# Hybrid encoder layer: first weight units, keys and six rounds of the expert choice moved into the stages before them

## The reference, cut to what matters

```python
proj = _rmsnorm(x, norm_mix) @ w_in            # GLA q, k, v, gate, decay codes; attention q, k, v; z_a, z_b
o_a = _gla_branch(...)                         # 4 heads, forward and backward scans in chunks
o_b = _gqa_branch(...)                         # 8 query heads, 2 key/value heads, softmax
merged = sigmoid(z_a) * (o_a @ w_o_gla) + sigmoid(z_b) * (o_b @ w_o_att)
x = x + merged @ w_out
h = _rmsnorm(x, norm_ffn)
aff = softmax(h @ w_router)                    # 16 experts, per group of tokens
gate_vals, idx = top_k(aff.T, cap)             # cap = 128 of the sample, 32 of the prompt
hid = silu(h[idx] @ w_e_gate) * (h[idx] @ w_e_up)
x = x.at[idx].add((hid @ w_e_down) * gate_vals)
```

## Time and profile before

| | |
|---|---|
| time, median of 3 runs (lowest to highest) | 3313.82 us (3312.66 to 3315.59) |
| the profiled execution: own time; its span | 3316.98 us; 3315.1 us |
| PE busy (matmuls) | 3036.5 us, 92% |
| DVE busy; ACT busy; POOL busy | 1709.4; 1522.0; 566.2 us |
| mean granted TensorE clock | 0.962 |
| DMA | 600.82 MB, mean 181 GB/s |

### The profile page before, as it was taken

How to read it: one execution, slowest core, us unless ns; L and a number is a source line. 1 busy time by engine, 2 the same in 40 slices (tenths; PEclk the granted TensorE clock), 3 DMA queues, 4 the chain that set the end, 5 groups by cost and what they waited for, 6 DMA issues and landing times. The chain is left out here.

```text
span 3315.1 us, 51547 instructions
## 1 busy us (share of the span) xinstructions
PE 3036.5 (92%) x19370; PEld 2396.8 (72%) x19370; DVE 1709.4 (52%) x1712; ACT 1522.0 (46%) x1635; POOL 566.2 (17%) x726
## 2 busy tenths in 40 slices
PE   7999998988888699979692999999999999999998
PEld 6888885766666589968572777777777777777776
DVE  3101001454432289942225767676676676666765
ACT  4211112445532166631342566665665565656654
POOL 0048881112220000000100011111100011111100
PEclk9999998999999799989895999999999999999999
DMA  4324322233215200024533788887777888878774
GB/s 153 122 98 142 119 89 96 84 100 103 90 61 179 92 20 19 13 91 144 173 127 129 267 296 288 285 298 272 280 279 287 298 287 285 302 272 297 277 280 155
DMA packets 196331, 600.82 MB, mean 181 GB/s; under 512 B 15184, under 2 KB 45536, under 8 KB 196256
## 3 DMA queue, kind: packets, MB, share of 16 engines
q1 hardware_dynamic: 165616, 506.46, 42.7%
q0 software_dynamic: 21920, 76.03, 7.7%
q10 hardware_dynamic: 8720, 17.30, 1.5%
HBM read 522.33 MB, written 77.33 MB: 181 GB/s over the span
## 5 line engine op out<-in xcount | busy, mean ns | idle before, releaser
L1871 DVE TENSOR_TENSOR ex_w_lo<-ex_w_raw,ex_w_hi 128x2048 fp32r<-128x2048 f32 x384 | 879.9, 2292 | 451.1 <-ACT ex_w_hi L1826 451.1
L1826 ACT ACTIVATE ex_w_hi<-ex_w_raw 128x2048 fp32r<-128x2048 f32 x381 | 729.9, 1916 | 469.6 <-PE ex_ps_s L1958 469.5
L1958 PE MATMUL ex_ps_s<-ex_w_hi,ex_xS 128*128 128x512 f32 x2048 | 578.2, 395 | 0.0
L1958 PEld LDWEIGHTS ex_ps_s<-ex_w_hi,ex_xS 128*128 128x128 f32 x2048 | 375.9, 188 | 99.4 <-issue 26.3
L1958 PE MATMUL ex_ps_s<-ex_w_lo,ex_xS 128*128 128x512 f32 x1024 | 316.4, 390 | 0.0
L1958 PE MATMUL ex_ps_s<-ex_w_hi,ex_hidS 128*128 128x512 f32 x1024 | 307.9, 403 | 0.0
L1812 POOL DMA_INDIRECT y<-ex_ye_s,ex_rows_y x16 | 43.5, 2717 | 1147.3 <-DVE ex_ye_s L1914 1147.3
L1969 PE MATMUL ex_ps_p<-ex_w_raw,ex_xP 128*32 128x256 f32 x4096 | 236.0, 383 | 0.0
L108 PE MATMUL pj_ps_tok<-pj_w_hi,act_hl 128*128 128x512 f32 x560 | 219.2, 391 | 8.6 <-DVE pj_w_lo L405 8.6
L1958 PEld LDWEIGHTS ex_ps_s<-ex_w_lo,ex_xS 128*128 128x128 f32 x1024 | 192.2, 188 | 41.4
L110 PE MATMUL pj_ps_tok<-pj_w_hi,act_hl 128*128 128x512 f32 x560 | 218.4, 390 | 0.0
(11 more groups left out here) (276 smaller groups left out, 5132.5 us busy)
## 6 DMA issues: line engine op xcount, KB each, us to landing
ex_w_raw<-w_e_gate SPq DMA_DIRECT2D x128, 1024.0 KB, 10.3
ex_w_raw<-w_e_up SPq DMA_DIRECT2D x128, 1024.0 KB, 12.5
ex_w_raw<-w_e_down SPq DMA_DIRECT2D x128, 1024.0 KB, 8.2
proj_t<-pj_stage SPq DMA_DIRECT2D x60, 256.0 KB, 2.0
pj_w_raw<-w_cols ACTq DMA_DIRECT2D x7, 2048.0 KB, 9.0
gl_z_w_raw<-w_z SPq DMA_DIRECT2D x16, 512.0 KB, 4.1
gate_logits<-gl_z_stage SPq DMA_DIRECT2D x32, 256.0 KB, 2.0
pj_w_raw<-x SPq DMA_DIRECT2D x10, 512.0 KB, 3.9
```

What stands on the lines that cost most here:

```text
L1826: act.activation(whl[0][:, j % NHL], raw[:, j % NRAW], ACT.Copy).then_inc(w_hi, 1)
L1871: dve.tensor_tensor(whl[1][:, j % NHL], raw[:, j % NRAW], whl[0][:, j % NHL].bitcast(F32), ALU.subtract).then_inc(w_lo, 1)
L1958: mm = pe.matmul(ps_s[:, s, c:c + 512], x(part, k), whl[w][:, j % NHL, kk, c:c + 512], start=k == 0 and part + w == 0, stop=k == 2 * PU - ...
```

## The change

- Units of 128 columns in `mix`, from weights that the host lays out so that one unit is one contiguous block. The first unit is loaded and split in the phase before: for `mg` in the last head of `gla` (in the buffers `zraw` and `zw`), for `ma` in `attention`. POOL's loads at the start of `mg` wait until six of eight row blocks are split (`rows_lo`).
- The phase `keys` is gone. Its work is done in `mg`, in five pairs of tiles, between the products.
- `w_out` is loaded from SP's queue behind the second store of `ma` (`follow`). In `finish_mixer` POOL's first issue is the first tile of `merged`, and its split stands between the second and the third unit of `w_out`.
- In `gla`, `soft_ln` of direction 1 goes from tile 8 to the end of the head, and the last wait of SP for `zw_lo` from tile 6 to tile 8 (`LATE_Z`). The gate weights are issued first.
- Six of the 16 rounds of the choice are done in `finish_mixer`: the sample's affinities are moved at tile 8, three rounds stand in tile 8 behind `hn`, one behind the residual add of tile 9, and two behind its `hn`. The prompt's affinities are moved in `choose` and take part in the last four rounds only.

```diff
@@ attention
+                sp.dma_start(w_unit[0].rearrange("p k c -> p (k c)"), w_next[0]).then_inc(w_landed, 16)
...
                 tiles(act, body)
+                act.wait_ge(w_landed, 16)
+                act.activation(w_unit[1], w_unit[0], ACT.Copy).then_inc(next_hi, 1)
                 for u in (2, 3):
                     out_high(NT - 1, u, TP)
...
                 tiles(dve, body)
+                dve.wait_ge(next_hi, CR + 1)
+                dve.tensor_tensor(w_unit[2], w_unit[0], w_unit[1].bitcast(F32), ALU.subtract).then_inc(next_lo, 1)
                 for u in (2, 3):
                     out_low(NT - 1, u, TP)
@@ mix, sync and gpsimd
+                for j in range(min(2, pairs_n)):
+                    load_kv(j)
+                for t, s in tiles:
                     sp.wait_ge(ready, CR + t + 1)
                     sp.dma_start(out[t * P:(t + 1) * P], o[:, s]).then_inc(stored[s], 16)
+                    if t == 1 and follow is not None:
+                        follow(sp)
+                    if 1 <= t < pairs_n - 1:
+                        load_kv(t + 1)
...
+                if source is not None:
+                    pool.wait_ge(rows_lo, CR + KC - 2)
+                for t, s in tiles:
+                    if t > 0:
+                        pool.wait_ge(w_lo, CR + max(t - 2, 0))
+                        pool.dma_start(raw[s].rearrange("p k c -> p (k c)"), w[t]).then_inc(w_in[s], 16)
+                    pool.wait_ge(gated, CR + t - 1)
+                    pool.dma_start(z[:, s], z_rows[t * P:(t + 1) * P]).then_inc(z_in[s], 16)
@@ mix, vector
+                for t, s in tiles:
+                    if t + 1 < NT8:
+                        low(t + 1, 1 - s)
...
+                    if 1 <= t <= pairs_n:
+                        key_rows(t - 1)
+                        value_low(t - 1)
+                    if 2 <= t <= pairs_n + 1:
+                        key_low(t - 2)
@@ mix, tensor
+                for t, s in tiles:
+                    pe.wait_ge(w_lo, CR + t)
                     pe.wait_ge(gated, CR + t - 1)
...
+                    if 1 <= t <= pairs_n:
+                        j = t - 1
+                        pe.wait_ge(normed, CR + j + 1)
+                        pe.wait_ge(k_lo, CR + j - 1)
+                        for h in range(KVH):
+                            for n in range(2):
+                                tr = pe.transpose(ps[:, j % 2, 3, (2 * h + n) * P:(2 * h + n + 1) * P], kr[:, j % 2, n, h], cst["ident"])
@@ gla, sync
+                        if t == LATE_Z and not last:
+                            more_z(ZC // 3 - 1)
+                        if t == 3 and last:
+                            sp.wait_ge(zw_lo, CR + NZ)
+                            sp.dma_start(zraw[:].rearrange("p k c -> p (k c)"), w_next[0]).then_inc(next_in, 16)
...
                 ph.start(sp)
+                gate_weights(0)
                 load_z(0)
                 sp.dma_start(A[:, 0], masks.rearrange("m p n -> p m n")).then_inc(const_in, 16)
-                gate_weights(0)
@@ gla, scalar
-                            if t == 8:
-                                soft_ln(i + 1, 1)
...
                     z_at("end")
+                    if not last:
+                        soft_ln(i + 1, 1)
                     turned(NT - 1)
@@ new
+def top_eight(dve, step, count, vals, lists, idx, r, rows):
+    v8, i8, done = lists[0:rows, 0, r * 8:r * 8 + 8], idx[0:rows, r * 8:r * 8 + 8], CR + 3 * count
+    dve.wait_ge(step, done)
+    dve.max(v8, vals[0:rows]).then_inc(step, 1)
+    dve.wait_ge(step, done + 1)
+    dve.max_index(i8, v8, vals[0:rows]).then_inc(step, 1)
+    dve.wait_ge(step, done + 2)
+    dve.match_replace(vals[0:rows], v8, vals[0:rows], -1.0).then_inc(step, 1)
@@ finish_mixer
-                for u in range(NU):
-                    sp.dma_start(raw[:, u], w_d[:, :, u * WC:(u + 1) * WC]).then_inc(w_in[u], 16)
...
+                    if ends_sample(n):
+                        sp.wait_ge(cleared, CR + 3)
+                        sp.wait_ge(a_out, CR + n)
+                        for j in range(2):
+                            sp.dma_start(vals[32 * j:32 * j + NE], affT[:, j * TS // 2:(j + 1) * TS // 2]).then_inc(aff_in, 16)
...
+                merged_in(0, 0)
                 pool.dma_start(gamma[:], norm_ffn.to_broadcast([P, D])).then_inc(c_in, 16)
...
+                    if last(n, 1):
+                        rounds(3, 4)
                     dve.wait_ge(rooted, CR + n + 1)
...
+                    if ends_sample(n):
+                        dve.wait_ge(aff_in, 32)
+                        rounds(0, 3)
+                    elif last(n, 1):
+                        rounds(4, EARLY)
@@ choose
-                for r in range(CS // 8):
...
+                for r in range(EARLY, CS // 8):
+                    if r == (CS - CP) // 8:
+                        dve.wait_ge(moved_in, 16)
+                    top_eight(dve, step, r - EARLY, vals, lists, idx, r, SAMPLE_ROWS if r < (CS - CP) // 8 else ROWS)
@@ program
+            def load_w_out(sp):
+                for u in range(4):
+                    sp.dma_start(w_out_raw[:, u], dram["w_out"].rearrange("(k p) c -> p k c", p=P)[:, :, 2 * P * u:2 * P * (u + 1)]
+                                 ).then_inc(w_out_in[u], 16)
```

More of the change, by code:

```diff
@@ L793, in mix @@
         stored = ph.stored("stored", 2)
-        w_d = w.rearrange("(k p) c -> p k c", p=P)
-        NU, PU = D // WC, WC // P
         ready = summed if add is not None else gated
         NT8 = D // P
-        units = [(u, u % 2) for u in range(NU)]
-        tiles = [(t, t % 2, t // PU, t % PU) for t in range(NT8)]
+        tiles = [(t, t % 2) for t in range(NT8)]
+        two = lambda t, j: t[:, :, 2 * P * j:2 * P * (j + 1)]
         with nc.Block() as block:
@@ L856, in _ @@
+                if keys is not None:
+                    dve.wait_ge(root_done, CR + 2)
+                    dve.reciprocal(inv[:], root[:]).then_inc(inverted, 1)
                 if source is not None:
@@ L1533, in body @@
                     act.activation(hT[:], ps_h[:], ACT.Copy).then_inc(h_out, 1)
-                    if not first(n):
+                    if not first(n) and not ends_sample(n):
                         aff_out(n - 1)
@@ L1557, in _, with rounds @@
                     dve.tensor_tensor(whl[1][:, :, cols], raw[:, u], whl[0][:, :, cols].bitcast(F32), ALU.subtract).then_inc(w_lo, 1)
+                    if u == 1:
+                        low(0, 0)
                 low(1, 1)
                 dve.wait_ge(c_in, 32)
+                dve.memset(vals[:], -1.0).then_inc(cleared, 1)
+                dve.memset(lists[:], 0.0).then_inc(cleared, 1)
+                dve.memset(idx[:], 0).then_inc(cleared, 1)
+                def rounds(a, b):
+                    dve.wait_ge(cleared, CR + 3)
+                    for r in range(a, b):
+                        top_eight(dve, step, r, vals, lists, idx, r, SAMPLE_ROWS)
                 def body(n, s, i):
@@ L2049, in _ @@
                 dve.wait_ge(eps_set, 3)
+        w_out_in = [nc.alloc_semaphore(f"w_out_in{u}") for u in range(4)]
+        z_bufs, out_stage = ExitStack(), ExitStack()
         with ExitStack() as mixer:
```

264 lines of the change are left out of this document (130 added, 134 removed).

## The result

The changed kernel takes 3242.6 us (median of 4 runs, 3239.4 to 3244.4), beside 3314.7 us for the kernel before on the same chip (4 runs): ratio 0.978, 95% interval 0.976 to 0.980. The forecast was 3232, range 3219 to 3248. The profiled execution took 3243.4 us with a span of 3241.8; its span is 73.3 us shorter than that of before, where the sum had said 81.9.

The account below looks back on a forecast made before the run. PE, busy nine tenths of the span, was taken as the bound, so only its standing stretches counted. Terms 16.7 + 6.5 + 16.4 + 8.7 + 16.8 + 16.8 = 81.9 us gave 3232 us, range 3219 to 3248.

Parts of the forecast that it names:

- Start of `gla`: At the start of `gla`, two issues of about 0.5 us move behind the gate weights: cost 0, bounds 0 and 1.
- Heads: In `gla`, k turns 5.8 us earlier in each of three heads, last head charged 0.7: together 16.7 us gained.
- Start of `mg`: PE starts `mg` earlier but waits for its second unit, held back by POOL: 6.5 us gained, bounds 2 and 9.5.
- Keys: The keys' phase, 19.9 us, goes; transposes cost 3.0 back and attention's load beside the first query load 0.5: 16.4 gained.
- Start of `ma`: PE starts with the phase, winning 10.2 us, less 1.5 for a split ahead of attention's last outputs: 8.7.
- `w_out`: `finish_mixer` starts earlier as the 4 MB load hides in `ma`: 16.8 us gained, bounds 13.9 and 17.5.
- Choice: Six rounds moved into `finish_mixer` win 13.8 us, the affinities' copy no longer preceding the first round 3.00: 16.8.
- the first: Rival for heads, `mg` and `merged`: chains move without closing, heads win 3 each; gain 66.7, time 3247; chance 0.15.
- The second: Rival: heads close fully and PE's second `mg` tile follows the first; gain 98, time 3215; chance 0.10.
- transfers rival: Two rivals: `w_out` and unit loads bind `ma`, 3282, chance 0.03; slower weight transfers bind the experts, 3359, chance 0.03.
- The sign set for it: Forecast wrong if an `mg` or `ma` product tile exceeds 14.5 us, or PE stands over 15 us in the experts.
- Short waits: At PE's remaining waits, even short ones, slow first matmuls follow: 2.47 us for six against 1.34 later.

Follow-up runs that it names:

- the two edits together: Changed kernel with gains on their own semaphore, second z unit ahead of v, gate rows and gains, and attention's weight unit held until the first query tile is scaled: 3235.5 us.

## Why the prediction came out as it did

Most of the mechanism held; the gain was 8.6 us smaller on the spans, 73.3 for 81.9 (8.3 on the executions' own times, 3243.4 for 3235.1), and the point 10.6 us too low. 2.4 of these 10.6 come from turning one execution into a median: that of before was 3.2 above its median, that of after 0.8.

- **Start of `gla`: the step that failed.** "the first z product waits for later loads too, so I take 0, bounds 0 and 1." It lost 5.1 us. 1.1 of them is the projection's end, which came later in each of the 12 edited kernels too, by 0.3 to 1.9 us, with the projection's code unchanged; its cause stays open. The other 3.9 lie from there to the first turn of k: 49.1 us against 45.2. How much of it is the change and how much the execution stays open: in the eight kernels with the same code there the loss is 0.6 to 3.9, against one execution of before. I had followed only PE's next wait and not the chain behind it on ACT and DVE: masks and gains, split of the first z unit, the second z unit, exponential and logarithm. The runs show that transfers bound it: with the second unit ahead of v, gate rows and gains it is 40.8. What they don't support is that the new order of loads is the culprit, since the old one gives back only 1.0 of it, less than the spread. In the old order's trace the second unit came 0.7 us later than before, PE stood 2.6 us, not 2.1, and a z product at half clock followed. Why the loads land some tenths to 2 us later than before wasn't settled; the tensors of z lie elsewhere in SBUF, which was not tried.
- **Heads: 16.9 for 16.7, in part by luck, and by a mechanism that was told too simply.** The three heads won 15.2, 5.1 each for the 5.8 forecast. The last head, charged with 0.7, won 1.7: its clock was high in this execution. In the eight other kernels with the same code in the heads the whole stretch won 11.7 to 15.3 against the same execution of before. k turned 11.3 us after the last turn, 11.05 forecast, with DVE's log gate as releaser. It turned late because the logarithm and DVE's work behind it are a chain of their own, as forecast. But the sum priced two edits as one chain. Moving the logarithm alone is worth 4.0 of the 5.1 us a head, moving the z load alone all of them; what one leaves the other adds.
- **Start of `mg`: 5.35 for 6.5 by the second tile's start, and 3.7 with what follows it.** PE starts where it was said (7.0 us after the issue), and waits 3.1 of the 4 us. But the second tile starts 21.7 us after the first, not 20.5: the first takes 18.6 us without the wait, not 16.5. And the 1.7 us at 1.2 GHz behind the wait, which before had none there, fall behind that mark. The first tile was quick in this execution, too: 21.7 us for 22.2 to 23.6 in the others with the hold. The hold, which I had priced as what makes the second unit late, is neutral.
- **Keys: 14.1 for 16.4.** The phase's 19.9 us went. The transposes cost 1.6, not the 3.0 taken and less than the lower bound of 2.4; the 1.7 us of slow clock of `mg` are the rest of what its products got longer by. The mis-sized term the other way is "Attention's SP load stands beside the first query load: 0.5 (bounds 0 and 1.5)": it measured 2.0. That load is also issued 6.3 us after the last product of `mg`, 0.6 more than the keys' first instruction was before. Booked by its cause, the term is 15.8 for 16.4.
- **Start of `ma`: 9.1 for 8.7.** From attention's last product to the first of `ma` 3.6 us are left of 13.4, and `ma` itself is 0.6 us longer. The split ahead of the last outputs, priced at 1.5, cost nothing that shows: attention is as long as before.
- **`w_out`: 16.2 for 16.8.** The first `merged` tile took 5.8 us to land; I took the splits of two units of `w_out` as the later bound. ACT's copy of the tile began at 1543.85 after 2.5 us of waiting for it, so landing was the bound. `w_out` itself is 14.5 of it, and its cover in `ma` holds.
- **Choice: 17.0 for 16.8.** Ten rounds of 2.30 us remain, and `finish_mixer` is 0.1 us longer.
- **Rivals.** Three terms of the first were tried by the trace: the heads won 5.1 us each and not 3, the start of `mg` 3.7 to 5.35 and not 2, the `merged` tile landed in 5.8 us and not 8.8. Each lies between forecast and rival. That the time is nearer to its 3247 than the point is has another main reason, the start of `gla`, which no rival named. (Its first term is short by 0.6: three times 5.8 less 3 is 8.4, not 7.8. The upper bounds add up to 97, not 96. Neither changes the argument.) The second didn't happen, since `k_product` holds PE as its counter-argument said. The experts are as long as before to 0.4 us, and the tiles of `ma` behind the first take 14.1 us each, as before, so neither transfers rival did. The sign set for it, a tile above 14.5 us, was drawn too close: tiles of `mg` with transposes took 14.4 to 14.5, and its second, which began at 1.2 GHz behind the wait that the sum had priced, 15.9.
- **Short waits.** "Each stretch that stays, even a short one, keeps this cost": not so for the shortest. After waits of up to 2.1 us at the start of `gla` the clock stayed at 2.4 GHz, and behind 3.0 us before the second tile of `mg` it stayed there in one execution and fell in others.

## What to carry to other kernels

Where two engines' chains meet in one stretch, undo each edit alone and both: here either edit of the heads brings back most of what the two bring together, and a price put on one of them by itself would have been wrong. Before a start of a phase is priced at nothing, follow the chain behind the first wait through every load that shares its semaphore or its queue; counting two loads on one semaphore held a copy of 0.3 us back by 9 us, and a unit asked for 8 us sooner landed only 2 us sooner until it also stood ahead of the bulk loads. Read a gain of 2 to 5 us in its own stretch, since the granted clock moves the same code by 3 us elsewhere, and read the stretch in more than one execution: here one alone would have confirmed a term of 16.7 that others put at 12 to 15. And choose a mark behind the slow clock of a wait, not in front of it, or its price is booked to the next term.

## What was not expected of the hardware

- A load's issue can take as long as a transfer: the broadcast of the gains over 128 partitions kept SP 4.22 us in the changed kernel and 2.9 to 4.2 in all others with the gate weights first, but 0.97 us in the kernel before and 0.85 with the old order of loads. What in the order does it isn't shown. Four loads of 1 MB kept SP 13.85 us in the run with `w_out` late and 10.98 in `ma` of the changed kernel.
- PE's clock after short waits: after 0.6 to 2.1 us of standing for ACT's copy at the start of `gla` (five executions) the next z product ran at 2.4 GHz; after 2.3 to 5.6 us (nine) it ran in part at 1.2 GHz. But waits of one length don't have one price: before the second tile of `mg` PE stood 2.97 us with the second z unit ahead, and the granted clock stayed at 1.00; with the two edits together it stood 3.03 us, and 5.8 us at 0.50 followed. The same 5.2 us before the last head's turn of k was followed by 39.8 us at 0.94 once, and by 41.0 to 43.5 us in eight other executions.
